# The delta rule of a two-block transformer kernel, unrolled over all eight heads

## The reference

```python
L = jnp.where(strict, jnp.einsum('bhnid,bhnjd->bhnij', k_beta, kc) * decay, 0.0)
T = lax.linalg.triangular_solve(eye + L, jnp.broadcast_to(eye, L.shape),
                                left_side=True, lower=True, unit_diagonal=True)
v_corr = jnp.einsum('bhnij,bhnjd->bhnid', T, v_beta)
k_cumdecay = jnp.einsum('bhnij,bhnjd->bhnid', T, k_beta * jnp.exp(gc)[..., None])
attn_intra = jnp.where(tril, jnp.einsum('bhnid,bhnjd->bhnij', qc, kc) * decay, 0.0)

def step(state, inp):
    q_i, k_i, v_i, kcd_i, g_i, a_i = inp
    v_new = v_i - jnp.einsum('bhcd,bhde->bhce', kcd_i, state)
    o = (jnp.einsum('bhcd,bhde->bhce', q_i * jnp.exp(g_i)[..., None], state)
         + jnp.einsum('bhij,bhje->bhie', a_i, v_new))
    g_last = g_i[..., -1]
    k_w = k_i * jnp.exp(g_last[..., None] - g_i)[..., None]
    state = state * jnp.exp(g_last)[..., None, None] + jnp.einsum('bhcd,bhce->bhde', k_w, v_new)
    return state, o
```

## Time and profile before

| What | us |
|---|---|
| median of 3 runs | 3687.05 |
| lowest and highest run | 3686.0, 3687.36 |
| the profiled execution, its own time | 3682.3 |
| its span in the trace | 3680.5 |
| TensorE busy | 2907.5 (79% of the span) |
| VectorE busy | 1861.8 (51%) |
| GpSimd busy | 1144.4 (31%) |
| ScalarE busy | 900.9 (24%) |

### The profile page before, as it was taken

One profiled execution on the slowest core, in us unless ns is written; L12 is line 12 of the kernel. 1 busy time (PEld: TensorE's weight loads), 2 busy tenths in 40 slices (PEclk: granted clock), 3 DMA queues, 4 the chain that ended last, 5 costly groups with the idle time before them and its releaser, 6 DMA issues. The chain is left out here.

```text
span 3680.5 us, 31683 instructions
## 1 busy us (share of the span) xinstructions
PE 2907.5 (79%) x10976; PEld 1922.4 (52%) x10976; DVE 1861.8 (51%) x3370; ACT 900.9 (24%) x1628; POOL 1144.4 (31%) x1200
## 2 busy tenths in 40 slices
PE   6999879997698897777799884767566857676777
PEld 5886668655575676767687762323222323232232
DVE  5753543334334463343524456667466557654443
ACT  2122221523256463121232321111011111111110
POOL 0000000000000131233100006666666666666664
PEclk8999989998899998998899997888888878887787
DMA  6541222101220122000122329999999999999997
GB/s 225 180 152 57 80 70 92 58 12 35 91 81 12 59 69 85 1 0 0 35 96 90 129 69 372 369 365 364 389 369 366 357 383 359 366 373 386 358 373 301
DMA packets 228465, 702.01 MB, mean 191 GB/s; under 512 B 23156, under 2 KB 25460, under 8 KB 227703
## 3 DMA queue, kind: packets, MB, share of 16 engines
q0 software_dynamic: 147456, 536.94, 37.6%
q1 hardware_dynamic: 80888, 163.56, 13.0%
HBM read 692.03 MB, written 8.39 MB: 190 GB/s over the span
## 5 line engine op out<-in xcount | busy, mean ns | idle before, releaser
L2544 DVE CUSTOM_DVE_ANT_0 proj_banks<-u_rows,work_banks 128x1024 f32<-128x1024 f32 x512 | 620.9, 1241 | 345.3 <-DMA u_rows<-in_peer_u_dram,eidx 221.9
L2629 PE MATMUL work_banks<-v_rows,diag 128*128 128x512 f32 x1024 | 512.1, 654 | 251.6 <-issue 153.9
L2525 POOL DMA_INDIRECT u_rows<-in_peer_u_dram,eidx x512 | 484.3, 946 | 571.8 <-DVEq L2574 416.1
L2629 PEld LDWEIGHTS work_banks<-v_rows,diag 128*128 128x128 f32 x1024 | 211.3, 209 | 550.2 <-issue 496.7
L218 DVE TENSOR_TENSOR weights_low<-weights_raw,weights_high 128x2048 fp32r<-128x2048 f32 x108 | 249.6, 2312 | 489.4 <-ACT weights_high L213 480.4
L2629 PE MATMUL work_banks<-x_res,diag 128*128 128x512 f32 x512 | 270.6, 681 | 199.1 <-issue 115.8
L276 PE MATMUL proj_banks<-h_low,weights_high 128*128 128x512 f32 x896 | 359.2, 401 | 31.2 <-DVE weights_low L218 12.9
L213 ACT CAST weights_high<-weights_raw 128x2048 fp32r<-128x2048 f32 x108 | 205.9, 1906 | 638.4 <-PE proj_banks L276 616.7
L276 PE MATMUL proj_banks<-h_high,weights_high 128*128 128x512 f32 x896 | 353.4, 394 | 0.0
L276 PE MATMUL proj_banks<-h_high,weights_low 128*128 128x512 f32 x896 | 353.0, 394 | 0.0
L2629 PEld LDWEIGHTS work_banks<-x_res,diag 128*128 128x128 f32 x512 | 109.1, 218 | 358.2 <-issue 269.6
(11 more groups left out here) (443 smaller groups left out, 4644.2 us busy)
## 6 DMA issues: line engine op xcount, KB each, us to landing
weights_raw<-in_w_in_dram SPq DMA_DIRECT2D x36, 1024.0 KB, 5.1
weights_raw<-in_ret_w_in_dram SPq DMA_DIRECT2D x24, 1024.0 KB, 5.3
ret_gate<-in_mod_w_dram SPq DMA_DIRECT2D x20, 1024.0 KB, 8.3
weights_raw<-in_fox_w_in_dram SPq DMA_DIRECT2D x16, 1024.0 KB, 5.5
weights_raw<-in_ret_w_out_dram SPq DMA_DIRECT2D x8, 1024.0 KB, 5.0
weights_raw<-in_peer_w_q_dram SPq DMA_DIRECT2D x8, 1024.0 KB, 5.1
u_rows<-in_peer_u_dram,eidx POOLq DMA_INDIRECT x512
ret_v<-in_mod_w_dram SPq DMA_DIRECT2D x4, 1024.0 KB, 13.5
```

The source lines that it names most:

```text
L2525: nc.gpsimd.indirect_dma_start(out=ur[:, s, e, :] if table is u_tab else v_row(s, e), out_offset=None, in_=table, in_offset=bass.IndirectO ...
L2544: nc.vector.tensor_tensor_reduce(out=trash[:, e % 2, :], in0=ur[:, g % 2, e, :], in1=hp, scale=1.0, scalar=0.0, op0=ALU.mult, op1=ALU.add, ...
L2629: last = nc.tensor.matmul(pa[:, half, :], diag[:, s, e, :], v_row(s, e)[:, half * CW:(half + 1) * CW], start=(first and e == 0), stop=(las ...
```

## The change

The loop over pairs is gone; the code of all eight heads is written out.

- Preparation runs over heads 0 to 7, and each engine works ahead: the decay rows of head h+2 are formed behind the products of head h. The staging copies are gone: PE and ACT read `qkv` and `sc` where they are, and the scaled v is written over v. `att` and `kw` are kept for all heads, `low` fills `x`.
- Inversion runs over two groups of four heads. In level 0, where the inverse is still the identity, PE only transposes the couplings (four products per head with the identity), and DVE forms both halves of `inv` from the transposed and the plain couplings. In level 6 only one half is formed, and DVE writes it to `low`. Heads share two pairs of `pb` banks in turn.
- Recurrence runs over 32 steps, chunk by chunk and in a chunk head by head, so eight chains alternate. PE issues for step n the products with the state, for step n-4 the outputs, and for step n-2 the new values. Banks rotate: three for the products with the state, two for the new values, three for the outputs. The products with the state are left out for chunk 0, and the state's addition for chunk 3. ACT takes over the scaled queries.
- Memory: `osb` is lent to the stage. Its content is stored to DRAM (`o_away`) in `delta_inputs` and loaded back at the start of `merge`, ahead of the weights there. The second halves of `whi` and `wlo` are lent too.
- `delta_gate` reads the output in another layout, same sizes.

```diff
@@ delta_inputs, SP @@
                     load(sp, then, 0, g0 + n)
+                    sp.dma_start(o_away, osb[:, :, :]).then_inc(o_put, 16)
                     sp.wait_ge(z_kept, 2 * TT)
                     sp.dma_start(z_away, zg[:, :, :]).then_inc(z_put, 16)
                     sp.wait_ge(z_put, 16)
+                    sp.wait_ge(o_put, 16)
@@ delta_rule, GpSimd @@
-                    with rounds(pool, H2) as p:
...
+                    def couplings(g, lv):
+                        for i in range(HG):
+                            if lv == 0:
+                                pool.wait_ge(prep_read, HG * g + i + 1)
+                                if g:
+                                    pool.wait_ge(y_full, nth(g - 1, LV - 1, i))
+                            elif lv == 1:
+                                pool.wait_ge(inv_ready, nth(g, 0, i))
+                            else:
+                                pool.wait_ge(y_full, nth(g, lv - 1, i))
+                            nc.gpsimd.tensor_tensor(cs[:, i, :, :], low[:, HG * g + i, :, :], masks[:, lv, :]
+                                                    .unsqueeze(1).broadcast_to([P, TT, P]), ALU.mult
+                                                    ).then_inc(cs_ready, 1)
+
+                    widen_g(0)
+                    widen_b(0)
+                    widen_g(1)
                     pool.wait_ge(masks_loaded, 16)
+                    for h in range(H):
+                        mask_decay(h)
+                        if h:
+                            widen_b(h)
+                        if h + 2 < H:
+                            widen_g(h + 2)
@@ delta_rule, TensorE @@
+                    def products(h):
+                        if h:
+                            pe.wait_ge(prep_read, h)
                         for c in range(TT):
                             cc = slice(c * P, (c + 1) * P)
+                            nc.tensor.matmul(pb[:, 1, cc], kh(h, c), kh(h, c), start=True, stop=True)
+                            nc.tensor.matmul(pb[:, 2, cc], kh(h, c), qh(h, c), start=True, stop=True)
+                        pe.wait_ge(wide_b_ready, h + 1)
+                        for c in range(TT):
+                            last = nc.tensor.matmul(pb[:, 0, c * P:(c + 1) * P], wide_b[:, c, :], ident,
+                                                    start=True, stop=True)
+                        last.then_inc(products_full, 1)
...
+                    def corrections(g, lv):
+                        for i in range(HG):
+                            pe.wait_ge(y_read, nth_y(g, lv, i))
+                            pe.wait_ge(inv_ready, nth(g, lv, i - 2) if i >= 2 else nth(g, lv - 1, i + 2))
...
+                    def state_products(n):
+                        c, h = n // H, n % H
+                        pe.wait_ge(state_ready, n - H + 1)
+                        if n >= H + 3:
+                            pe.wait_ge(u_ready, n - H - 2)
+                            pe.wait_ge(qs_ready, n - H - 2)
...
+                    decay_rows(0)
+                    decay_rows(1)
+                    for h in range(H):
+                        products(h)
+                        tokens(h)
+                        if h + 2 < H:
+                            decay_rows(h + 2)
+                    for g in range(NG):
+                        coupled(g, 0)
+                        for lv in range(1, LV):
+                            coupled(g, lv)
+                            corrections(g, lv)
+                    for n in range(TT * H + 4):
+                        if H <= n < TT * H:
+                            state_products(n)
+                        if n >= 4:
+                            outputs(n - 4)
+                        if 2 <= n < TT * H + 2:
+                            new_values(n - 2)
@@ delta_rule, VectorE @@
+                    def first_inverse(g):
+                        for i in range(HG):
+                            dve.wait_ge(y_full, nth(g, 0, i))
+                            if g:
+                                dve.wait_ge(inv_ready, nth(g - 1, LV - 1, i))
+                            each = ident.unsqueeze(1).broadcast_to([P, TT, P])
+                            nc.vector.tensor_tensor(inv[:, i, :, 0, :], each, chunks(pa[:, i, :]), ALU.subtract)
+                            nc.vector.tensor_tensor(inv[:, i, :, 1, :], each, cs[:, i, :, :], ALU.subtract
+                                                    ).then_inc(inv_ready, 1)
@@ merge, SP @@
+                    sp.dma_start(osb[:, :, :], o_away).then_inc(o_back, 16)
                     load_chunks(sp, columns(a["w_in_2"][0], 7 * D + 2 * GDN_HEADS), 2 * n, w_sb)
+                    sp.wait_ge(o_back, 16)
```

More of the change, by code:

```diff
@@ new lines, in products, with tokens @@
+                        last.then_inc(products_full, 1)
+                    def tokens(h):
+                        if h:
+                            pe.wait_ge(tok_read, h)
+                        for c in range(TT):
+                            cc = slice(c * P, (c + 1) * P)
+                            nc.tensor.transpose(pa[:, 2, cc], kh(h, c), ident)
+                            last = nc.tensor.transpose(pa[:, 3, cc], vb(h, c), ident)
+                        last.then_inc(tok_full, 1)
@@ new lines, in inverse, with last_inverse @@
+                    def inverse(g, lv):
+                        for i in range(HG):
+                            dve.wait_ge(z_full, nth_y(g, lv, i))
+                            for half in range(2):
+                                part = inv_flat[:, i, half, :]
+                                last = nc.vector.tensor_tensor(part, part, pb[:, 2 * (i % 2) + half, :], ALU.subtract)
+                            last.then_inc(inv_ready, 1)
+                    def last_inverse(g):
+                        for i in range(HG):
+                            dve.wait_ge(z_full, nth_y(g, LV - 1, i))
+                            nc.vector.tensor_tensor(low[:, HG * g + i, :, :], inv[:, i, :, 1, :],
+                                                    chunks(pb[:, 2 * (i % 2), :]), ALU.subtract).then_inc(inv_ready, 1)
@@ L2153, in delta_gate @@
+                    for n in range(TT * H + 2):
+                        if H <= n < TT * H:
+                            scaled_queries(n)
+                        if n >= 2:
+                            keep_new_values(n - 2)
     def delta_gate(qkv, ogt, z_away):
```

422 lines of the change are left out of this document (221 added, 201 removed).

## The result

| What | before | after |
|---|---|---|
| median of 4 runs each, us | 3687.2 | 3549.05 |
| lowest and highest run | 3686.0, 3694.72 | 3543.55, 3553.53 |
| the profiled execution, its own time | 3682.3 | 3543.55 |
| its span in the trace | 3680.5 | 3541.1 |

The change is worth 138.2 us: the time is 0.962 of that before, with a 95% interval of 0.9606 to 0.9635. The forecast was 3551.5 us, 2.4 us above the median.

What follows compares the result with a forecast made beforehand. The delta rule stage was taken as bound by TensorE's products, waits and the recurrence's chain. Preparation 46, inversion 139, recurrence 36 and clock 3 sum to 224 us against 359.5, giving 3551.5 us, range 3533 to 3594.

Steps and rivals of the forecast that it cites:

- cold spell: Delta rule stage: one spell of some 5 us at low TensorE clock costs 2.5 us; 3 us added, bounds zero and 10.
- The period of 5.1 us: Preparation: heads follow at 5.1 us, from 2.7 us of products, 2.16 us of VectorE with hand-over, and 0.2 us.
- start-up: Preparation's beginning: widenings, decay rows at low clock, first products, VectorE's first reading and hand-overs take 10.2 us.
- The level of 10.7 us: Inversion with four heads: a full level has 48 products and takes 10.7 us, its waits met before.
- the place 0.15 us wide: Inversion: head 2's corrections need bank 0 back after 1.6 us, while head 1's corrections fill 1.8 us; the tightest place.
- turn-taking: Inversion, levels 0 to 1: GpSimd and VectorE's SBUF-only operation alternate, 2.1 us per head, four heads per group.
- The last level: Inversion's end: 16 + 16 products, 7.2 us, and 0.6 us of bank waits.
- The 3 us for two or three semaphores per group: Recurrence: product groups wait on two or three semaphores instead of one; 3 us taken, between 0 and 19 us.
- The rival at 1.2 GHz throughout: Whole stage: TensorE stays at the low clock, 388 us against 359.5, kernel 3716 us; chance 0.02.
- Both moves of 2 MB at zero: Outside the stage: o_sb's store before it and load back in merge are covered, zero cost; uncovered, 15 us together.
- The rival of a transfer that shows: Outside the stage: both 2 MB moves are exposed, +15 us, kernel 3567 us; chance 0.05.
- z_away to be issued at the same moment: Before the stage: sign that z_away's transfer is issued at the same moment as in the kernel before, 1438.81 us.

Runs made afterwards that it cites:

- early_banks: Changed kernel with preparation's first eight products of the next head waiting only for VectorE's first two operations, the last four for the third: 3379.95 us, stage 212.3 us.
- psum_input: Changed kernel with level 0's second VectorE operation reading the PSUM bank instead of the identity (wrong values): 3381.66 us in a single run, stage 214.1 us.
- recur2: Changed kernel with only the recurrence put back to two chains, heads two at a time: 3552.43 us, 0.9648 of before, stage 231.6 us.
- noloan: Changed kernel without the store and load of o_sb, so merge's first branch reads other values: 3535.01 us, 0.9609 of before, stage 217.6 us.
- level0: Changed kernel with level 0 of the inversion computed like the other levels, 64 products more: 3550.2 us, 0.9645 of before, stage 228.2 us.
- own_buffer: Changed kernel with level 1's couplings written to buffer ys, so GpSimd need not wait for VectorE: 3383.78 us in a single run, stage 214.2 us.
- changed_again: Changed kernel once more, no edit, on another chip beside a kernel before of 3525.83 us: 3388.57 us, 0.9611 of before, stage 217.6 us.

## Why the prediction was right

**The sum.** The stage took 217.4 us where the sum had 224. By its terms:

| Term | forecast | measured | from |
|---|---|---|---|
| preparation | 46 | 47.9 | 1453.2 to 1501.1 |
| inversion | 139 | 136.7 | 1501.1 to 1637.8 |
| recurrence | 36 | 32.8 | 1637.8 to 1670.6 |
| cold spell | 3 | 0.9, within the inversion's 136.7 | 18.6 us for levels 0 and 1, 17.7 at full clock in early_banks |

**Preparation.** The period of 5.1 us was right (5.11), and so was its cause: early_banks takes the single release away and 0.67 us per head go. The start-up was longer than the 10.2 us. 47.9 less 7 x 5.11 leaves 12.1, and in it TensorE waits 2.35 us for ScalarE before the inversion, which the sum did not have: I had looked at who reads the product banks, and not at ScalarE's eight scalings per head that read the transposes' banks.

**Inversion.** The level of 10.7 us was exact (10.72), and the place 0.15 us wide held. The rest is in the turn-taking: 1.89 us per head (1507.80 to 1509.69 for the couplings) where I had 2.1. GpSimd ends at 1507.75 and VectorE's operation, issued at 1506.92, at 1508.29, 0.54 us later; GpSimd's next begins at 1508.37. So a turn is 1.27 + 0.54 + 0.08: VectorE's 0.68 us end 0.54 us behind GpSimd, and my sum counted them in full. The mechanism was right and its size 0.2 us too large. The sum also had four such turns per group, and there are three: behind GpSimd's fourth multiplication stands no VectorE operation, so that one takes 1.3 us and not 2.1. Level 0 to the last correction of level 1 came to 18.6 and 17.6 us against 18.95. The 18.6 us have the cold spell in them, so both groups stand 1.3 us below the sum, and the two errors of the turns are 0.6 and 0.8 us of it. The last level took 7.36 us against 7.8. psum_input shows the contention itself: about 2 us per group.

**Recurrence.** The chain was hidden fully: 1.1175 us per step, five products of 0.2235 us. The 3 us for two or three semaphores per group was the term that was mis-sized: seven satisfied waits per step cost TensorE nothing that the trace can show. recur2 shows that what was removed is the chain (3.37 us per chunk of two heads).

**Clock.** One cold spell came, but not where I looked for it: not in the bursts of level 0, where TensorE paused 0.43 to 0.74 us at each turn and the second group still ran at 1.00, but behind the 2.35 us wait for ScalarE. The 16 products there take 1.6 us longer, but VectorE and GpSimd taking turns set the pace behind them, and the stage loses only 0.9 us of the 3. What makes the clock fall there stays open: early_banks has the same wait and kept the full clock. The rival at 1.2 GHz throughout fell. The Trainium skill ("TensorE: Matmul & The Clock Gate", section "A second HAM failure mode: psum-queue depth-cycling") has micro-idles between groups that cycle through PSUM banks make the clock swing; by that rule the turns of level 0 should have made it swing, and the trace does not agree: the clock granted is 1.00 in both groups' turns.

**DMA.** Both moves of 2 MB at zero were right (noloan). The rival of a transfer that shows is out. In merge the fourth sigmoid starts 24.2 us after the first load, where it was 22.6; in noloan, without the fetch, it is 24.6, so those 1.6 us are not the fetch's, and what they are is not shown.

**Outside the stage.** This I had wrong in its details: I expected z_away to be issued at the same moment, and it came 6.8 us later (1445.65). The trace places that at the program's very start, long before the change. TensorE's rows of the kernel before, and then of the changed one:

```profile
22.23 8.90 PE L645 MATMUL proj_banks<-mod_cols,ret_v 128*128 128x1 f32 x64
...
40.81 0.53 PE L276 MATMUL proj_banks<-h_high,weights_low 128*128 128x512 f32 x1
```

```profile
23.55 11.06 PE L661 MATMUL proj_banks<-mod_cols,ret_v 128*128 128x1 f32 x64
...
46.83 0.42 PE L292 MATMUL proj_banks<-h_high,weights_low 128*128 128x512 f32 x1
```

The same 32 products (x64 in the trace) take 11.06 us instead of 8.90, and the products behind them run at the lower clock, 0.63 us each, until 46.8 us instead of 40.8. From the rows shown on they take 0.39 us. The first load behind 45 us is issued at 68.66 instead of 62.04 us. The code there is the same. In the other profiled kernels that load stands at 62.1 to 68.2 us (62.2 in level0 and noloan, 68.15 in early_banks), and at 68.7 and 68.6 in the two profiled executions of the changed kernel. Whether the placement of code decides it or chance, these runs do not tell, and I leave it open. So the forecast of 3551.5 us, 2.4 us from the median, owes part of its closeness to luck: the stage gained 7 us more than I had said, and the rest of the program lost 3.3. Within those 3.3 us the late start and the shorter expert layer nearly cancel, and neither was forecast.

## What to carry to other kernels

In a stage with barriers at both ends, count the products and ask of every wait how far back it looks: with a look-back of a few steps a chain of engines disappeared under TensorE here, and its satisfied waits cost nothing. Split a stage into its parts before and after, too: half of this gain came from a part with a fifth of the products, in which TensorE waited most. Beside a GpSimd multiplication from SBUF, a VectorE operation with both inputs in SBUF took double the time here (1.37 us for 0.68); give it one input in PSUM, or a moment when GpSimd is idle. Read the gain from the stage's own boundaries, because the start of the program alone moved by 6.6 us without an edit.

## What the runs showed of the hardware

- Satisfied semaphore waits cost TensorE nothing visible: a recurrence step with five products and seven waits lasts 1.1175 us, 5 x 0.2235.
- Either of VectorE and GpSimd can be the one that the contention lengthens. In the changed kernel GpSimd's multiplication began 0.4 us ahead at each turn and stayed at 1.27 us (at most 1276 ns), while VectorE's 128x512 subtraction grew from 0.68 to 1.37 us. In own_buffer there is a place where the two begin within 0.02 us of each other (1507.29 and 1507.31): GpSimd's takes 1.83 us there, VectorE's 0.68.
- A pause of TensorE of 2.35 us was followed by 3 us at the lower clock in the changed kernel, and the same pause in early_banks by none. Pauses of 0.43 to 0.74 us at the turns, of 1.30 us in the preparation and of 1.48 us in level0 were not followed by the lower clock.
- When TensorE's clock rises at the start of the program differs by 6 us between kernels that are the same there.
- The changed kernel's stage takes 217.4 us in the result's profile and 217.6 us in changed_again, on a chip where the whole kernel is faster. The kernel before takes 3687.2 us there and 3525.83 here, 4% apart, and nearly all of such a difference is in the expert layer: 1637.2 us in the changed kernel of the result against 1481 in changed_again.
